# Seven more low parts per second mixer on GpSimd, in a float32 transformer stack on one core

## The reference, cut to what matters

```
h = h + 0.5 * swiglu_2(rms_norm(h, ln_ffn1[l]), ffn1_w13[l], ffn1_w2[l])
u = rms_norm(h, ln_mix[l])
z, xbc, dt_raw, cq, ckv, kr, gates = split_cols(u @ w_in[l], IN_SPLIT_SIZES)
y_ssd = ssd_branch(z, xbc, dt_raw, ...)     # silu(conv(xbc)), a chunked state scan, gated by silu(z)
y_mla = mla_branch(cq, ckv, kr, ...)        # latent attention, 8 heads
g = sigmoid(gates)
h = h + (g[..., :D_MODEL] * y_ssd + g[..., D_MODEL:] * y_mla) @ w_o[l]
```

## Time and profile before

| | us |
|---|---|
| timed runs, median (lowest to highest) | 2789.8 (2786.63 to 2793.22) |
| profiled execution | 2786.49 |
| its span, first to last instruction | 2784.7 |
| PE busy in the span | 2721.8 |
| DVE busy | 1483.6 |
| ACT busy | 1345.4 |
| POOL busy | 662.4 |

### The profile page before, as it was taken

One profiled execution on the slowest core, in us unless ns is written; L12 is line 12 of the kernel. 1 busy time (PEld: TensorE's weight loads), 2 busy tenths in 40 slices (PEclk: granted clock), 3 DMA queues, 4 the chain that ended last, 5 costly groups with the idle time before them and its releaser, 6 DMA issues.

```text
span 2784.7 us, 32279 instructions
## 1 busy us (share of the span) xinstructions
PE 2721.8 (98%) x12892; PEld 2237.3 (80%) x12892; DVE 1483.6 (53%) x2246; ACT 1345.4 (48%) x1559; POOL 662.4 (24%) x153
## 2 busy tenths in 40 slices
PE   8999999999999999999999999999999999999999
PEld 7888778888887778888887787788888887877887
DVE  3438773333458763433358885443334488864433
ACT  4335664334345654343356574443433464744432
POOL 4330014444420023343410000043444100000333
PEclk9999999999999999999999999999999999999999
DMA  6554435556554345555544244355555542442553
GB/s 227 190 181 163 151 124 195 181 178 204 183 170 161 135 138 196 184 181 195 184 166 157 76 156 160 123 182 182 181 198 178 190 145 86 152 155 105 186 189 135
DMA packets 209928, 461.23 MB, mean 166 GB/s; under 512 B 9458, under 2 KB 31604, under 8 KB 209780
## 3 DMA queue, kind: packets, MB, share of 16 engines
q1 hardware_dynamic: 209780, 459.17, 48.5%
HBM read 458.09 MB, written 1.05 MB: 165 GB/s over the span
## 4 chain that ended last, share of the span: by engine, by line
PE 84%; DVE 9%; ACT 4%; issue 3%; POOL 0%; DMA 0%; DVEq 0%; ACTq 0%; SPq 0%
PE banks L322 26%; PE banks L324 25%; PE banks L323 25%; PE banks L416 3%; DVE w_lo L261 2%; ACT w_hi L285 2%; PE banks L659 2%; DVE xbcT L1718 1%; PE banks L682 1%; PE banks L1425 1%; PE banks L1439 1%; PE banks L671 0%; ACT h_hi L446 0%; DVE h_lo L460 0%; POOL w_lo L261 0%
## 5 line engine op out<-in xcount | busy, mean ns | idle before, releaser
L285 ACT ACTIVATE w_hi<-raw 128x2048 fp32r<-128x2048 f32 (+1 forms) x441 | 832.9, 1889 | 1151.4 <-PE banks L324 1102.5
L261 POOL TENSOR_TENSOR w_lo<-raw,w_hi 128x2048 fp32r<-128x2048 f32 (+1 forms) x141 | 648.0, 4596 | 1725.5 <-ACT w_hi L285 1725.5
L261 DVE TENSOR_TENSOR w_lo<-raw,w_hi 128x2048 fp32r<-128x2048 f32 (+1 forms) x300 | 692.8, 2314 | 609.7 <-ACT w_hi L285 602.7
L322 PE MATMUL banks<-w_hi,h_lo 128*128 128x512 f32 x2336 | 924.6, 396 | 13.5 <-DVE w_lo L261 6.3
L324 PE MATMUL banks<-w_hi,h_hi 128*128 128x512 f32 x2336 | 909.1, 389 | 0.0
L323 PE MATMUL banks<-w_lo,h_hi 128*128 128x512 f32 x2336 | 908.5, 389 | 0.0
L322 PEld LDWEIGHTS banks<-w_hi,h_lo 128*128 128x128 f32 x2336 | 441.9, 189 | 116.7 <-issue 16.2
L324 PEld LDWEIGHTS banks<-w_hi,h_hi 128*128 128x128 f32 x2336 | 441.1, 189 | 91.2
L323 PEld LDWEIGHTS banks<-w_lo,h_hi 128*128 128x128 f32 x2336 | 441.7, 189 | 84.6
L322 PE MATMUL banks<-w_hi,act_lo 128*128 128x512 f32 x704 | 276.3, 392 | 0.9 <-POOL w_lo L261 0.9
L324 PE MATMUL banks<-w_hi,act_hi 128*128 128x512 f32 x704 | 274.4, 390 | 0.0
(11 more groups left out here) (272 smaller groups left out, 2544.7 us busy)
## 6 DMA issues: line engine op xcount, KB each, us to landing
raw<-in_ffn_w SPq DMA_DIRECT2D x124, 1024.0 KB, 5.0
raw<-in_w_in SPq DMA_DIRECT2D x108, 1024.0 KB, 5.0
raw<-in_ffn_w_down SPq DMA_DIRECT2D x44, 1024.0 KB, 4.8
raw<-in_ffn_w_gate SPq DMA_DIRECT2D x40, 1024.0 KB, 5.0
raw<-in_ffn_w_up SPq DMA_DIRECT2D x40, 1024.0 KB, 5.0
raw<-in_w_ssd_out SPq DMA_DIRECT2D x16, 1024.0 KB, 4.9
raw<-in_w_branch SPq DMA_DIRECT2D x8, 1024.0 KB, 4.8
raw<-in_w_out SPq DMA_DIRECT2D x8, 1024.0 KB, 4.8
```

The source lines that it names most:

```text
L261: eng.tensor_tensor(w_lo[:, c % SPLIT, 0:kc * n], raw[:, c % RAW, 0:kc * n], w_hi[:, c % SPLIT, 0:kc * n].bitcast(F32), ALU.subtract).then ...
L285: self.eng.activation(w_hi[:, c % SPLIT, 0:kc * n], raw[:, c % RAW, 0:kc * n], ACT.Copy).then_inc(hi_made, 1)
L322: pe.matmul(ps, al, bh, start=first, stop=False)
```

## The change

A second list of makers is used for the two second mixers: chunks 5, 7, 9, 11, 13, 15 and 17 of each go from VectorE to GpSimd, beside chunk 1, which GpSimd had before. Nothing else changes; the places at which DVE issues low parts stay, and skip those chunks.

```diff
+        def mixer2_makers(chunks):
+
+            return ["GV"[c not in (1, 5, 7, 9, 11, 13, 15, 17)] for c in range(len(chunks))]
+
...
-            makers += ffn_makers(ffns[0]) + mixer_makers(mixer) + ffn_makers(ffns[1])
+            makers += ffn_makers(ffns[0]) + (mixer_makers, mixer2_makers)[KINDS[L]](mixer) + ffn_makers(ffns[1])
```

## The result

The changed kernel takes 2800.28 us, the median of 6 runs (2797.70 to 2803.72), against 2789.82 for the kernel before (6 runs). The ratio is 1.0036, with a 95% interval of 1.0025 to 1.0046: about 10 us slower. The profiled execution took 2800.99 us, its span 2799.2.

A forecast was written before the change was run, and what follows sets the result against it. DVE's order of work, on which PE waits, was taken as the bound. Per mixer 2.2 + 1.2 - 0.65 = 2.75, with the clock 4.35; twice, +8.7 us, gave a median of 2798.5, range 2790 to 2806.

The forecast's parts named there:

- Two low parts exclude each other: DVE ops with all operands in SBUF stand still until GpSimd's low part (4.6 us) is done, and the reverse.
- Chunks 8 and 9, 2.2 us: GpSimd's low part 9 holds up DVE's low part 8, so PE starts chunk 8 2.2 us late; bounds 0 and 3.7.
- Chunks 12 and 13, 1.2 us: GpSimd's low part 13 holds up DVE's low part 12, so CB, which PE waits for, comes 1.2 us later.
- Chunk 17, a gain of 0.65: Low part 17 leaves DVE ahead of the last convolution, which starts 0.65 us earlier, then limited by ACT's taps.
- DMA: Chunk 8's buffer is refilled 2.9 us later, but the transfer still lands 0.8 us before its high part starts.
- The clock, 1.6 us per mixer: New PE gaps of 2.0 us and 1.8 us (at CB) cause one short fall to 1.2 GHz per mixer, 1.6 us.
- the prediction's sign: To show it right: granted clock of the 26 us from 1462, in the first front, under 1.00.
- Chunks 5, 7, 11 and 15 at nothing: Low parts 5, 7, 11 and 15 on GpSimd delay nothing; if this cover is missing, one more delay of 2.2 us.
- (a): Rival: same delays in the fronts, but the clock holds at 2.4 GHz; +5.5 us, 2795.3; chance 0.24.
- (b): Rival: the clock falls at both new gaps or for the long stretch; 12 to 16 us more, 2802 to 2805; chance 0.13.
- (c): Rival: no exclusion worth naming, DVE reaches low parts 8 and 12 first or both overlap; -2.6 us, 2787.2; chance 0.06.
- (d): Rival: the buffers' two chunks of lead take up GpSimd's longer op, nothing moves; 2790 us; chance 0.07.

The follow-up runs named there:

- e6: Changed kernel, but GpSimd's chunks 9, 11 and 13 wait for DVE's low parts 8, 10 and 12; 2786.8 us, ratio 0.9990 to the kernel before.
- e3: Against the kernel before, only chunk 9 of each second mixer moves to GpSimd; 2800.1 us, ratio 1.0031.
- e9: Against the kernel before, only chunk 13 of each second mixer moves to GpSimd; 2792.6 us, ratio 1.0008.
- e7: Against the kernel before, only chunk 11 of each second mixer moves to GpSimd; 2799.9 us, ratio 1.0037.
- e2: Against the kernel before, even chunks 8, 10, 12, 14, 16 and 18 of each second mixer move to GpSimd; 2779.2 us, ratio 0.9956.
- e1: Changed kernel, but GpSimd's chunks 9 and 13 wait for DVE's low parts 8 and 12; 2799.2 us, ratio 1.0029 to the kernel before.
- e4: Changed kernel with chunks 9 and 13 back on DVE, GpSimd making 5, 7, 11, 15 and 17; 2797.8 us, ratio 1.0023 to the kernel before.
- e5: Changed kernel with chunks 9, 11 and 13 back on DVE, GpSimd making 5, 7, 15 and 17; 2788.7 us, ratio 0.9996 to the kernel before.
- e8: Against the kernel before, chunks 12, 16 and 18 of each second mixer move to GpSimd; 2777.8 us, ratio 0.9960.
- e11: Against the kernel before, only chunk 18 of each second mixer moves to GpSimd; 2781.5 us, ratio 0.9971.

## Why the prediction was right

Forecast 2798.5, measured 2800.3. By its own steps, in the profile of the changed kernel:

- *Two low parts exclude each other.* Right: low part 8 took 5.26 us and low part 12 5.64, each ending 2.15 us after GpSimd. e6 against the changed kernel shows that the order, not the load, makes the time.
- *Chunks 8 and 9, 2.2 us.* The start of chunk 8 moved from 1461.92 to 1465.20 while the front's start moved by 1.12: 2.16, with a wait of 2.00 as forecast. e3 shows it alone.
- *Chunks 12 and 13, 1.2 us.* CB's wait is 1.78 for the forecast 1.8, the delay 1.20. e9 shows it alone, 1.1 at that place.
- *Chunk 17, a gain of 0.65.* The last convolution moved by 3.94 when CB had moved by 4.48: 0.54.
- *DMA.* Hidden: high part 11 started when PE released its buffer.
- *The clock, 1.6 us per mixer.* The size was fair, in part by luck, for the place was half right. Behind the new 2.0 us gap the clock fell in the second front (1.6 us) and not in the first, where the 26 us from 1462 had 1.00 although the prediction's sign asked for less; behind the gap at CB it fell in neither. Not in the sum were the stretches at 1.2 GHz that stood at the end of the fronts before: they moved, and from the last convolution to the front's end another 1.25 us were lost in the first front and 0.9 in the second. Together the clock took 3.7 us, for the forecast 3.2. Both fronts together lost 9.4 us, the sum said 8.7.
- *Chunks 5, 7, 11 and 15 at nothing.* Right for this kernel. For chunk 11 the reason was wrong: it is free only because chunk 9's delay moves its high part behind DVE, by 0.8 us. Alone it costs 10 us in both mixers together (e7): PE starts chunk 10 3.15 us later in each, and in the first a stretch at 1.2 GHz right behind costs another 1.6. The one further delay of 2.2 us that I had named for a missing cover was too small. I had not looked at the copy of sums and its 32-element op ahead of low part 10.

What the agreement hides is that the terms do not add. 9, 11 and 13 alone lengthen the fronts by 5.9, 10.0 and 4.1 us, all together by 9.4: each delay decides who comes first at the next meeting. I worked through chunk 11 with 9's delay in place, and that kept the sum right.

Of the rivals, (a) and (b) differ from the forecast in the clock alone: it took 3.7 us, where (a) has none and (b) 6.8 to 10. The argument for (b), small PE ops in the 6.8 us stretches, doesn't tell them apart: two of the 3.4 us stretches before (1765.0 and 2543.2) have them as well. (c), DVE first everywhere, is what e6 builds: forecast 2.6 us less than before, measured 2.9 (interval 0.3 to 5.3). Rival (d), nothing moves, is excluded by e3 alone.

## What to carry to other kernels

Before giving GpSimd an op on SBUF beside a busy DVE, list for each instance what DVE does in its 4.6 us. Ops that read a bank go on; a TENSOR_TENSOR or TENSOR_SCALAR with all operands in SBUF stops, even one of 32 elements, and what stands behind it in the queue comes late with it (no other kind with all operands in SBUF stands in the count below). Choose the instances that fall under long bank-reading ops and whose removal shortens a chain on which PE waits (here 12, 16 and 18), or hold GpSimd back with a wait on DVE's last such op; by count and by busy share, the losing set and the winning one look alike (DVE 53% and GpSimd 26% in the changed kernel, 52% and 26% in e2). When you take out one meeting, look at the next one again: a delay can be its cover.

## What the runs showed that I had not expected

- The rule has no exception in the 14 profiles. I took the DVE ops that began while a GpSimd op had 0.3 us or more to go. All 263 with all operands in SBUF were stretched, and each full low part among them (232) ended 2.14 to 2.16 us after GpSimd's op. Of some 3500 that read a bank none was.
- A 128x32 TENSOR_TENSOR of 0.19 us took 3.4 to 3.6 us beside GpSimd's low part (e1, e4, e7), and a 128x64 TENSOR_SCALAR with one tensor operand 4.62 instead of 0.19.
- An old PE gap can keep 2.4 GHz in one execution and lose it in another: the gaps of 3.06 us near 295 and 1.88 us near 1796 kept it in the profile before and lost it in the changed kernel's. So a profile's span alone can be off by several us between kernels; the fronts' own lengths agree better where I can compare (253.6 us before, 252.5 in e5, whose medians differ by 1; 243.1 in both e2 and e8).
- Taking 2.2 us off a chain on DVE gave 3.7 to 3.9 us per front (e11), the rest coming with fewer stretches at 1.2 GHz: in the first front PE is 2.5 us ahead at 1533.6 of the kernel before, inside its last such stretch (1529.5 to 1536.3), and 3.5 us at 1535.9.
